# Block attention: the four tiles of key weights and the two tiles of memory-key weights take a 512-column product in place of two 256-column ones

## What is computed

```python
def moba_attention(h, w_q, w_o, cos, sin, k_blk, v_blk, k_mean):   # 8 heads of 128, 256 tokens: one block of 256 keys
    q = apply_partial_rope((h @ w_q).reshape(bsz, seq, N_HEADS, HEAD_DIM_2), cos, sin)
    ...
    s_own = jnp.einsum("bhqd,bhkd->bhqk", q_c, k_own) * scale
    s_own = jnp.where(kpos[None, :] <= qpos[:, None], s_own, -jnp.inf)
    p = jax.nn.softmax(...)
    o = jnp.einsum("bhqk,bhkd->bhqd", p, v_own)
    return out @ w_o

# k, v = split(rms_norm_2(x, kv_norm) @ w_kv), and the keys get the partial rope too
# memory attention of layer 1: k, v = split(rms_norm_2(mem, norm_memkv[1]) @ mem_w_kv[1])
```

## Time and profile before

| | us |
|---|---|
| median of 3 runs | 1240.38 (1239.78 to 1240.83) |
| the profiled execution's own time | 1240.27 |
| its span | 1238.5 |

### The profile page before, as it was taken

How to read it: one execution, slowest core, us unless ns; L and a number is a source line. 1 busy time by engine, 2 the same in 40 slices (tenths; PEclk the granted TensorE clock), 3 DMA queues, 4 the chain that set the end, 5 groups by cost and what they waited for, 6 DMA issues and landing times.

```text
span 1238.5 us, 18082 instructions
## 1 busy us (share of the span) xinstructions
PE 1228.5 (99%) x7432; PEld 1094.5 (88%) x7432; DVE 927.9 (75%) x1291; ACT 659.1 (53%) x873; POOL 31.1 (3%) x23
## 2 busy tenths in 40 slices
PE   8999999999999999999999999999999999999998
PEld 7888889978888888888888888889998888888887
DVE  7786766878777858988568777659978657877744
ACT  6665544456555444546546555445555445555632
POOL 0000000000000000440000000000000000000000
PEclk9999999999999999999999999999999999999999
DMA  9565764234555663556336555654445533555560
GB/s 324 184 217 174 233 206 156 83 137 165 187 192 184 203 228 134 180 194 208 133 136 231 188 193 183 224 170 148 159 140 183 189 136 137 204 199 180 194 210 34
DMA packets 51426, 221.74 MB, mean 179 GB/s; under 512 B 4464, under 2 KB 5776, under 8 KB 30864
## 3 DMA queue, kind: packets, MB, share of 16 engines
q1 hardware_dynamic: 51056, 220.25, 51.9%
q10 hardware_dynamic: 288, 0.33, 0.1%
HBM read 219.52 MB, written 1.05 MB: 178 GB/s over the span
## 4 chain that ended last, share of the span: by engine, by line
PE 92%; DVE 5%; ACT 1%; issue 1%; DMA 1%; SPq 0%; DVEq 0%; ACTq 0%
PE bank L418 48%; PE bank L462 21%; PE bank L422 7%; PE bank L449 5%; PE bank L507 2%; DVE wt L1273 2%; PE bank L761 2%; PE bank L789 2%; PE bank L484 1%; PE bank L510 1%; PE bank L489 1%; DMA raw<-weights 1%; PE bank L777 0%; PE bank L544 0%; DVE xn L1282 0%
## 5 line engine op out<-in xcount | busy, mean ns | idle before, releaser
L1273 DVE TENSOR_TENSOR wt<-raw,wt 128x2048 fp32r<-128x2048 f32 x202 | 464.1, 2299 | 68.0 <-ACT wt L916 67.5
L916 ACT ACTIVATE wt<-raw 128x2048 fp32r<-128x2048 f32 x202 | 386.0, 1911 | 121.7 <-PE bank L422 87.7
L418 PE MATMUL bank<-xn,wt 128*128 128x512 f32 x1712 | 416.4, 393 | 2.7 <-DVE xn L1282 1.5
L418 PEld LDWEIGHTS bank<-xn,wt 128*128 128x128 f32 x1712 | 313.1, 188 | 64.4 <-DVE xn L1282 2.1
L418 PE MATMUL bank<-h,wt 128*128 128x512 f32 x1004 | 246.2, 392 | 0.0
L462 PEld LDWEIGHTS bank<-xn,wt 128*128 128x128 f32 x1824 | 234.2, 191 | 9.7 <-DVE wt L1273 0.8
L462 PE MATMUL bank<-xn,wt 128*128 128x256 f32 x1824 | 238.2, 283 | 0.2 <-DVE wt L1273 0.2
L418 PEld LDWEIGHTS bank<-h,wt 128*128 128x128 f32 x1004 | 182.6, 188 | 34.1 <-issue 0.4
L1378 DVE TENSOR_TENSOR scratch<-bank,rest 128x512 f32<-128x512 f32 x98 | 67.6, 690 | 86.9 <-ACT rest L928 86.8
L999 ACT ACTIVATE h<-scratch 128x256 fp32r<-128x256 f32 x88 | 36.7, 418 | 158.8 <-DVE scratch L1418 158.8
L928 ACT ACTIVATE rest<-bank 128x512 f32<-128x512 f32 x114 | 67.6, 593 | 65.6 <-PE bank L462 64.1
(11 more groups left out here) (226 smaller groups left out, 971.0 us busy)
## 6 DMA issues: line engine op xcount, KB each, us to landing
raw<-weights SPq DMA_DIRECT2D x158, 1024.0 KB, 4.9
raw<-weights SPq DMA_DIRECT2D x88, 512.0 KB, 5.3
raw<-weights SPq DMA_DIRECT2D x8, 256.0 KB, 4.3
k_t<-mem_t SPq DMA_DIRECT2D x2, 1024.0 KB, 8.1
raw<-weights SPq DMA_DIRECT2D x8, 128.0 KB, 4.0
out_t<-work SPq DMA_DIRECT2D x4, 256.0 KB, 2.3
x<-x_t SPq DMA_DIRECT2D x3, 256.0 KB, 5.3
v_s<-fourier SPq DMA_DIRECT2D x2, 256.0 KB, 5.1
```

Source lines behind the costliest of these rows:

```text
L418: return pe.matmul(out, hi, a.rearrange("p a s -> p (a s)"), start=first, stop=False, skip_group_check=True)
L916: act.activation(wt[t % RING][:, 0], raw[t % RING][:], ACT.Copy).then_inc(weight_hi, 1)
L1273: dve.tensor_tensor(wt[t % RING][:, 1], raw[t % RING][:], wt[t % RING][:, 0].bitcast(F32), ALU.subtract).then_inc(weight_lo, 1)
```

## The change

NARROW becomes a list of single tiles: the five tiles of w_in, and of the block attention only the queries and values. k0, k1, k2, k3, m0 and m1 become wide, and so pass through `rest` on ACT and `whole_of` on DVE. The first tile of the stage also gets the cuts (4, 6) that first tiles of other wide stages have.

```diff
-NARROW = ("w_in", "moba")
+NARROW = [("w_in", j) for j in range(5)] + [("moba", j) for j, (what, _) in enumerate(MOBA) if what in "qv"]
...
-        if _name not in NARROW:
+        if (_name, _j) not in NARROW:
             REST[_name, _j] = len(RESTS)
             RESTS.append((_name, _j))
...
-                    value_tile(t, out, src, ks=ks, beside=more.get("beside", {}), narrow=kind in NARROW)
+                    value_tile(t, out, src, ks=ks, beside=more.get("beside", {}), narrow=(kind, j) in NARROW)
                 else:
-                    square_tile(t, out, src, ks=ks, narrow=kind in NARROW, **more)
+                    square_tile(t, out, src, ks=ks, narrow=(kind, j) in NARROW, cuts=(4, 6) if "late" in more else (), **more)
...
             def rest_part(kind, j):
                 what, i = PARTS[kind][j]
-                if kind == "moba":
+                if (kind, j) in NARROW:
                     src = pair_banks(kind, j)
...
             def scaled(name, j, dst, r):
-                if name in NARROW:
+                if (name, j) in NARROW:
```

## The result

| | before | after |
|---|---|---|
| median of 14 runs each, us | 1240.26 (1239.78 to 1240.89) | 1242.48 (1241.95 to 1243.3) |
| the profiled execution's own time, us | 1240.27 | 1242.79 |
| its span, us | 1238.5 | 1241.0 |

The ratio is 1.0017, with a 95% interval of 1.001 to 1.0024: 2.2 us slower, and 1242.4 had been forecast.

What follows compares the result with a forecast made beforehand. TensorE, busy 92% of the span, was taken as the bound, with DVE a second bound hidden by its lead. 2.42 us of lag less 0.26 of gain gave +2.16 on 1240.27, so 1242.4; own range 1241.9 to 1243.0, with rivals 1240.8 to 1243.9.

Steps and rivals of the forecast that it cites:

- A wide tile saves 0.19 us: TensorE, block attention: 16 products of 512 columns replace 32 narrow ones, saving 0.19 us a tile, 1.1 us for six.
- DVE is later by 1.34 us after k1 and 2.85 after k3: DVE, key tiles: one more addition each, 0.72 us, less 0.1 for the factors' spread, plus 0.05 at k2.
- ACT's copies cost nothing: ACT, wide tiles: one more 0.59 us copy a tile, costed at nothing because something later arrives last.
- Meeting points: Where TensorE waits for DVE or ACT: lags of 0.8 us at scores(0), 1.1 at out(2), 1.5 at out(3), 2.4 at out(4).
- The copy of v2 is the last meeting point: At out(4), TensorE waits for ACT's copy of v2: lead 0.60 us, lag 2.4 us, nothing delayed further behind it.
- m0 gains 0.07 and m1 0.19: Behind out(4), TensorE's wide memory-key tiles still count: 0.07 us for m0's last six products, 0.19 for m1.
- The cuts cost or save nothing: Tile k0: the operand's last pairs are ready in time, and a wait there before scores(0) would cost nothing.
- The stage's sum: Block attention as a whole: 2.42 us of lag less 0.26 of gain, +2.16 us.
- the second (ACT): Rival: ACT's copies of k2 and k3 come on the path, 0.59 us each; +3.4 us, 1243.6; chance 0.18.
- the third (the lead holds): Rival: DVE's additions hide and TensorE keeps all its gains, 1.1 us; 1239.2; chance 0.06.
- The first: Rival: DVE regains some between 902 and 908 us, so only out(3)'s lag stays; +1.3 us, 1241.6; chance 0.13.
- The fourth: Rival: new waits drop TensorE's clock to 1.2 GHz for a tile; +5.6 us more, 1248; chance 0.03.

Runs made afterwards that it cites:

- no_rest_v2: The change with the wide tiles' second halves never read (coarser output) and ACT's copy of v2 ahead of head 6's exponentials: 1239.14 us, ratio 0.9991.
- dve_spare: The kernel before, all tiles narrow, plus one DVE addition into a spare buffer behind each of k0 to k3: 1242.44 us, ratio 1.0017.
- act_spare: The kernel before, all tiles narrow, plus ACT's six copies into a spare buffer: 1240.18 us, ratio 0.9998.
- v2_first: The whole change, with ACT's copy of v2 moved ahead of the exponentials of head 6: 1241.58 us, ratio 1.0012.
- k_only: The change for the four key tiles k0 to k3 only, m0 and m1 narrow as before: 1242.64 us, ratio 1.0019.
- k3: The kernel before with only tiles k3, m0 and m1 made wide, without the cuts: 1240.41 us, ratio 1.0002.
- m_only: The kernel before with only the memory-key tiles m0 and m1 made wide: 1240.03 us, ratio 0.9997.
- pool_scale: The change, with the multiplication of k0 to k3 moved from DVE to POOL and the turning of k2 and k3 placed later: 1242.73 us, ratio 1.002.
- k3_v2: The kernel before with tiles k3, m0 and m1 wide, no cuts, and ACT's copy of v2 ahead of head 6's exponentials: 1240.09 us, ratio 0.9999.
- k23_v2: The kernel before with tiles k2, k3, m0 and m1 wide, no cuts, and ACT's copy of v2 ahead of head 6's exponentials: 1240.31 us, ratio 1.0.

## Why the prediction was right, point by point

1. *A wide tile saves 0.19 us.* k3 took 890.64 - 884.90 = 5.74 us where it had taken 5.95 (883.92 to 889.87): 0.21. The gain was right, not the lengths: 5.6 and 5.8 were forecast from tiles that stand elsewhere. k0 to k3 in no_rest_v2: 0.82 us by out(4), 0.2 each. The formula of the Trainium skill ("TensorE: Matmul & The Clock Gate", Back-to-back issue gap) would give an estimated 0.04 a tile; the measurement decides for the rows.
2. *DVE is later by 1.34 us after k1 and 2.85 after k3.* Measured 1.32 and 2.79, and dve_spare shows that this alone makes the loss. (The terms written down, 2.88 - 0.1 + 0.05, make 2.83; and the 0.05 for k2 is not there, since DVE did not wait for k2's copy.) The 0.1 taken off for the spread of the factors is seen too: less the start, DVE copied them 0.12 us earlier.
3. *ACT's copies cost nothing.* Shown by act_spare, and by a DVE that never waits for them ahead of out(4).
4. *Meeting points.* Lags at scores(0), out(2), out(3), out(4), as starts less 0.38: 0.72, 0.98, 1.46, 2.25 us. The prediction's 0.8, 1.1, 1.5 and 2.4 count the 0.11 of a restart, which shows only in what follows: one instruction group later the lags are 0.79, 1.06, 1.53 and 2.36. So the restart itself was 0.07 to 0.11 us. The profile gives TensorE a wait of 1.00 at scores(0), where 1.1 to 1.3 was forecast, and of 0.58 at out(4), not 0.7 to 1.0. That is two ways of counting: from start to start, with 0.120 us for each product before it, scores(0) was put off by 864.01 - 862.85 = 1.16 us and out(4) by 913.24 - 912.50 = 0.74; the profile counts from a modelled end that lies about 0.15 later.
5. *The copy of v2 is the last meeting point*, and what is gained ahead of it is lost. v2_first, k_only and k3 show both.
6. *m0 gains 0.07 and m1 0.19.* Together 0.20 in place of 0.26, in m_only and in the change alike. m0's first piece gained nothing, as foreseen.
7. *The cuts cost or save nothing, since a wait in k0 would lie before scores(0).* Wrong: without them the stage is 0.50 us longer. The step failed because it followed TensorE's queue only. The 0.8 us that k0 loses are passed on to DVE through the spread of the factors (0.48 us), and DVE brings them to every later meeting point. It did not show in the sum, because the change has the cuts and no such wait.
8. *The stage's sum*: 2.36 - 0.20 = 2.16 by the profile's places, 2.15 by its length, 2.42 - 0.26 = 2.16 forecast. That it fits to a hundredth is luck of two small errors, in points 4 and 6.

Of the rivals, the second (ACT) and the third (the lead holds) are refuted by act_spare and by the four waits. The first had the right order of places and one too few. The fourth, a fall of the clock, did not happen: 1.00 in all three stretches, with 1.0 and 1.25 us of waits in the first two, which is TensorE's 2.4 GHz level.

## What to carry to other kernels

A TensorE at 99% does not mean that the other engines are free. Where DVE has no idle time over tens of microseconds, look for each place where TensorE waits for it, directly or through ACT, and take the smallest lead as the price limit: here extra work under it was free, and above it everything counted, in full, once, with the restart on top (k3: 0.72 - 0.60 + 0.17 forecast, 0.28 measured). The same lead caps what TensorE can gain, so an edit that shortens its work and lengthens DVE's should be judged tile by tile by its place: behind the last meeting point it pays, and ahead of one where TensorE waits it is lost. Moving an instruction behind which nothing else can start (here ACT's copy of v2) ahead of a wait was worth 0.79 us in the change and 0.50 with k3, more than a wide product; it can pay only where TensorE waits at that place, and on the kernel before it was not run.

## What the runs showed of the hardware

POOL is not a free engine beside a busy DVE. A POOL multiplication from SBUF and a DVE instruction with two SBUF inputs did not run together in pool_scale. Whichever came second waited: DVE by 0.99 and 0.55 us, POOL by about 2 us behind one DVE subtraction. The Trainium skill ("SBUF — State Buffer", Who interferes with whom) says that a DVE instruction with two SBUF inputs contends with a GpSimd instruction that reads SBUF, and that the order of issue decides which of them blocks; the trace agrees. DVE's shuffle, with one input, kept its 0.73 us beside POOL, and POOL's multiplication for k3, which met only DVE instructions with at most one input in SBUF, took its 1.29 us.

Where profiles of one core are as repeatable as these, a stage's length between two fixed products tells 0.1 us apart, while the medians' intervals were 1.1 us to each side. In the six kernels that do the same up to scores(0) (before, m_only, act_spare, k3, k3_v2, k23_v2), it started 29.53 to 29.55 us after the stage; in three that do the same up to out(3) (the change, k_only, v2_first), out(3) started 72.02 to 72.08 us after it. The start of a stage 830 us into the kernel moved by 1.3 us between executions.
